# Two stacked blocks on one core: the recurrence's root as Ln and Exp on ScalarE, pieces of two gates exchanged, and x in the queue of the weights

## What is computed

```python
h = _rmsnorm(x, g_mix[l])                       # first block
y_xa = _memory_cross_attention(xa_q, _rmsnorm(mem, g_mem[l]), w_mem_kv[l], xa_g_q[l], xa_g_k[l])
...
for l in range(DEPTH_2):                        # second block
    h = x @ w_in[l]
    (hg_q, hg_f, hg_i, hg_gate, mla_cq, mla_ckv, mla_kr, mla_gate, mem_q, mem_gate) = jnp.split(h, IN_OFFSETS, axis=-1)
    ...
    y = jnp.concatenate([y_hg * jax.nn.silu(hg_gate), y_mla * jax.nn.silu(mla_gate), y_mem * jax.nn.silu(mem_gate)], axis=-1)
    x = _layernorm(DEEPNORM_ALPHA * x + y @ w_out[l], ln_g[l], ln_b[l])

# y_hg, with lb the layer's lower bound, 8 heads of 128
logf = jax.nn.log_sigmoid(z) + jnp.log1p(lb * jnp.exp(-z))
k = (1.0 - lb) * jax.nn.sigmoid(-z)
o = _chunk_gated_recurrence(q32, k, v, logf)    # v is hg_i
o = o * lax.rsqrt(jnp.mean(o * o, axis=-1, keepdims=True) + RMS_EPS)
```

## Time and profile before

| | us |
|---|---|
| median of 3 runs | 1149.06 (1148.51 to 1149.32) |
| the profiled execution | 1149.22, its span 1147.4 |
| PE busy | 1061.4 (93%) |
| DVE busy | 750.1 (65%) |
| ACT busy | 639.1 (56%) |
| granted PE clock, mean of the span | 0.966 of 2.4 GHz |

### The profile page before, as it was taken

The page is one execution under the profiler, slowest core; times in us unless marked ns, Lnnn a source line. Parts: engine busy times, 40 slices in busy tenths (PEclk is TensorE's granted clock), DMA queues, the critical chain, the costliest instruction groups (busy, mean ns, idle before and its releaser), DMA issues.

```text
span 1147.4 us, 19085 instructions
## 1 busy us (share of the span) xinstructions
PE 1061.4 (93%) x8070; PEld 943.4 (82%) x8070; DVE 750.1 (65%) x1070; ACT 639.1 (56%) x910; POOL 13.2 (1%) x18
## 2 busy tenths in 40 slices
PE   5799999999999999998999998896999999979975
PEld 4698987888879999987999997574899999957654
DVE  3575685885555878753646576669875564675786
ACT  4766565564464655543565678543356657784430
POOL 1000000000000000000000000100000000010000
PEclk9899998999999999999899999998999999998988
DMA  9553433566455565572546433222455463432110
GB/s 327 160 181 113 130 125 114 183 202 197 152 161 188 165 198 171 183 231 81 189 147 193 147 111 127 94 75 74 148 175 153 131 186 126 146 128 75 57 56 37
DMA packets 97688, 167.52 MB, mean 146 GB/s; under 512 B 7033, under 2 KB 32515, under 8 KB 97347
## 3 DMA queue, kind: packets, MB, share of 16 engines
q1 hardware_dynamic: 95216, 158.13, 43.1%
q0 software_dynamic: 1472, 5.51, 1.4%
q10 hardware_dynamic: 914, 2.67, 0.6%
HBM read 165.23 MB, written 1.05 MB: 145 GB/s over the span
## 4 chain that ended last, share of the span: by engine, by line
PE 80%; DVE 8%; ACT 7%; issue 2%; DMA 1%; ACTq 0%; DVEq 0%
PE proj L577 12%; PE proj L578 12%; PE proj L579 12%; PE proj L568 11%; PE proj L569 10%; PE proj L570 10%; ACT whi L985 2%; PE mix L881 1%; PE mix L590 1%; DVE arena L1895 1%; DVE wlo L1419 1%; PE mix L912 1%; PE mix L615 1%; PE mix L598 1%; ACT arena L1336 1%
## 5 line engine op out<-in xcount | busy, mean ns | idle before, releaser
L1419 DVE TENSOR_TENSOR wlo<-raw,whi 128x1024 fp32r<-128x1024 f32 (+3 forms) x303 | 355.1, 1202 | 198.6 <-ACT whi L985 197.2
L985 ACT ACTIVATE whi<-raw 128x1024 fp32r<-128x1024 f32 (+3 forms) x303 | 305.1, 1039 | 157.7 <-PE proj L579 70.7
L568 PE MATMUL proj<-act_hi,whi 128*128 128x256 f32 x1056 | 303.9, 288 | 7.8 <-DVE wlo L1419 4.2
L569 PE MATMUL proj<-act_lo,whi 128*128 128x256 f32 x1056 | 300.8, 285 | 0.0
L570 PE MATMUL proj<-act_hi,wlo 128*128 128x256 f32 x1056 | 300.8, 285 | 0.0
L568 PEld LDWEIGHTS proj<-act_hi,whi 128*128 128x128 f32 x1056 | 204.5, 194 | 9.8 <-DVE wlo L1419 4.4
L569 PEld LDWEIGHTS proj<-act_lo,whi 128*128 128x128 f32 x1056 | 204.6, 194 | 0.3
L570 PEld LDWEIGHTS proj<-act_hi,wlo 128*128 128x128 f32 x1056 | 204.5, 194 | 0.0
L577 PE MATMUL proj<-whi,y_hi 128*128 128x512 f32 (+1 forms) x352 | 141.9, 403 | 20.4 <-DVE X L1477 16.3
L578 PE MATMUL proj<-wlo,y_hi 128*128 128x512 f32 (+1 forms) x352 | 138.3, 393 | 0.0
L579 PE MATMUL proj<-whi,y_lo 128*128 128x512 f32 (+1 forms) x352 | 138.3, 393 | 0.0
(11 more groups left out here) (341 smaller groups left out, 1229.4 us busy)
## 6 DMA issues: line engine op xcount, KB each, us to landing
raw<-in_w_in SPq DMA_DIRECT2D x144, 512.0 KB, 4.4
raw<-in_w_up SPq DMA_DIRECT2D x88, 256.0 KB, 3.9
raw<-in_w_out SPq DMA_DIRECT2D x32, 512.0 KB, 3.6
raw<-in_w_down SPq DMA_DIRECT2D x22, 512.0 KB, 4.9
raw<-in_w_mem_kv SPq DMA_DIRECT2D x8, 512.0 KB, 9.4
raw<-in_w_mem_k SPq DMA_DIRECT2D x8, 512.0 KB, 3.8
raw<-in_w_o SPq DMA_DIRECT2D x8, 512.0 KB, 4.4
raw<-in_w_mem_v SPq DMA_DIRECT2D x8, 512.0 KB, 3.9
```

What stands on the lines that cost most here:

```text
L568: mm(o, wh[:, i, wc], hi[:, k0 + i, :], start=begin and j % 2 == 0, stop=False, skip_group_check=True)
L569: mm(o, wh[:, i, wc], lo[:, k0 + i, :], start=False, stop=False, skip_group_check=True)
L985: fn(whi[c % SPLIT][:, 0:w], raw[c % SLOTS][:, 0:w], ACT.Copy).then_inc(s.w_hi, 1)
L1419: tt(wlo[c % SPLIT][:, 0:w], raw[c % SLOTS][:, 0:w], f32(whi[c % SPLIT][:, 0:w]), ALU.subtract).then_inc(s.w_lo, 1)
```

## The change

Four things are moved, and one computation takes another form.

1. SP issues identity, mem, four pieces, x, and the other pieces; ACT issues the large constants only when x has landed, and POOL waits for x and no longer for mem. ACT squares mem behind piece 1 and x behind piece 3, and the first split before the root ends at piece 4.
2. hgi is projected ahead of hgg. hgi0 leaves its bank before the forget values' exponentials, hgi1 behind their Ln; hgg0 and hgg1 both leave in unit 3. |u| is formed on DVE in two halves (max of u and -u) behind the second latent output.
3. Keys 2 to 7 are made in pairs behind the splits of units 0 to 2.
4. mlaout1's first piece stands ahead of the last unit's products; gated(0) moves from unit 3 to unit 4; square(3) stands ahead of a split, and the split for mlaout1 on DVE behind both scales.
5. The root of the head norm is exp(-0.5 ln(.)) on ACT, for heads 0 to 3 within unit 6, and DVE only multiplies.

The diff, with context and empty lines left out:

```diff
@@ -147,7 +147,7 @@
                ("uk", [piece(a["w_mla_uk_2"][L], 0, 1, 0, 512)]), ("uv", [piece(a["w_mla_uv_2"][L], 0, 1, 0, 512)])]
-    groups += [(name, hg[name]) for name in ("hgf0", "hgf1", "hgq1", "hgg0", "hgg1", "hgi0", "hgi1")]
+    groups += [(name, hg[name]) for name in ("hgf0", "hgf1", "hgq1", "hgi0", "hgi1", "hgg0", "hgg1")]
@@ -494,10 +494,12 @@
         def _(sp):
+            sp.dma_start(const[:, 0:P], a["const"][:, 0:P]).then_inc(s.ident_in, 16)
+            for b in range(NB):
+                sp.dma_start(MEM[:, b, :], a["mem"][0, b * P:(b + 1) * P]).then_inc(s.mem_in, 16)
             for c, loads in enumerate(pieces):
-                if c == 1:
-                    for b in range(NB):
-                        sp.dma_start(MEM[:, b, :], a["mem"][0, b * P:(b + 1) * P]).then_inc(s.mem_in, 16)
+                if c == SLOTS:
+                    sp.dma_start(X[:, :, :], a["x"][0].rearrange("(b p) d -> p b d", p=P)).then_inc(s.x_in, 16)
                 if c >= SLOTS:
@@ -513,7 +515,7 @@
         def _(pool):
-            pool.wait_ge(s.mem_in, 32)
+            pool.wait_ge(s.x_in, 16)
             pool.dma_start(TREE_IN[:, :], a["tree"]).then_inc(s.tree_in, 16)
@@ -841,21 +843,21 @@
-                project("hgg0", L, act_hi, act_lo, part=(0, 1))
+                project("hgi0", L, act_hi, act_lo, part=(0, 1))
...
-                project("hgg0", L, act_hi, act_lo, part=(1, 2))
+                project("hgi0", L, act_hi, act_lo, part=(1, 2))
...
-                project("hgg0", L, act_hi, act_lo, part=(2, 4))
-                project("hgg1", L, act_hi, act_lo, part=(0, 2))
+                project("hgi0", L, act_hi, act_lo, part=(2, 4))
+                project("hgi1", L, act_hi, act_lo, part=(0, 2))
...
-                project("hgg1", L, act_hi, act_lo, part=(2, 3))
+                project("hgi1", L, act_hi, act_lo, part=(2, 3))
...
-                project("hgg1", L, act_hi, act_lo, part=(3, 4))
-                project("hgi0", L, act_hi, act_lo, part=(0, 3))
+                project("hgi1", L, act_hi, act_lo, part=(3, 4))
+                project("hgg0", L, act_hi, act_lo, part=(0, 3))
@@ -865,7 +867,7 @@
-                        project("hgi0", L, act_hi, act_lo, part=(3, 4))
+                        project("hgg0", L, act_hi, act_lo, part=(3, 4))
@@ -944,15 +946,16 @@
-                        project("hgi1", L, act_hi, act_lo, part=(u, u + 1))
+                        project("hgg1", L, act_hi, act_lo, part=(u, u + 1))
...
+                    if u == 7:
+                        project("mlaout1", L, y_hi, y_lo, 8, part=(0, 1))
...
-                project("mlaout1", L, y_hi, y_lo, 8, part=(0, 1))
@@ -1043,8 +1046,6 @@
-            act.dma_start(const[:, 0:P], a["const"][:, 0:P]).then_inc(s.ident_in, 16)
-            act.dma_start(X[:, :, :], a["x"][0].rearrange("(b p) d -> p b d", p=P)).then_inc(s.x_in, 16)
@@ -1057,21 +1058,23 @@
-            act.dma_start(const[:, P:], a["const"][:, P:]).then_inc(s.consts, 16)
...
-            split_until(SPLIT)
+            split_until(2)
...
+            split_until(SLOTS)
...
+            act.dma_start(const[:, P:], a["const"][:, P:]).then_inc(s.consts, 16)
...
+            split_until(SLOTS + 1)
@@ -1295,25 +1298,24 @@
-                split_until(ahead_of("hgg0", L, 1))
+                split_until(ahead_of("hgi0", L, 1))
...
-                leave("hgg0", L, HGT[:, 0:4, :], ACT.Silu)
+                split_until(ahead_of("hgi1", L, 0))
...
-                split_until(ahead_of("hgg1", L, 2))
+                split_until(ahead_of("hgi1", L, 2))
...
-                act.wait_ge(s.hg_u, L + 1)
+                leave("hgi0", L, HV[:, :, 0:512])
...
-                for h in quarter:
-                    last = fn(HX[:, h, :], HU[:, h, :], ACT.Abs)
-                link(last)
-                leave("hgg1", L, HGT[:, 4:8, :], ACT.Silu)
-                for h in quarter:
+                for n, h in enumerate(quarter):
+                    act.wait_ge(s.hg_u, 2 * L + n + 1)
...
+                nc.scalar.preload_act_table(ACT.Exp)
+                leave("hgi1", L, HV[:, :, 512:1024])
@@ -1355,42 +1357,55 @@
-                split_until(ahead_of("hgi0", L, 1))
+                def logs(dst, src):
+
+                    return fn(dst, src, ACT.Ln, bias=epsb[:, 0:1], scale=1.0 / HG_D)
+
+                def roots(dst):
+
+                    return fn(dst, dst, ACT.Exp, scale=-0.5)
+
+                split_until(ahead_of("hgg0", L, 1))
...
-                split_until(ahead_of("hgi0", L, 2))
+                split_until(ahead_of("hgg0", L, 2))
...
-                keys(2, 8)
-                leave("hgi0", L, HV[:, :, 0:512])
...
-                        split_until(ahead_of("hgi1", L, u))
+                        split_until(ahead_of("hgg1", L, u))
+                        keys(2 * u + 2, 2 * u + 4)
...
-                        leave("hgi1", L, HV[:, :, 512:1024])
+                        leave("hgg0", L, HGT[:, 0:4, :], ACT.Silu)
+                        leave("hgg1", L, HGT[:, 4:8, :], ACT.Silu)
+                        nc.scalar.preload_act_table(ACT.Exp)
...
+                    if u == 6:
+                        act.wait_ge(*out_of("hgo1", L))
+                        link(logs(HKT[:, 0:4, :], HKT[:, 0:4, :]))
+                        roots(HKT[:, 0:4, :]).then_inc(s.hg_r, 2)
...
-                root = lambda dst, src: fn(dst, src, ACT.Sqrt, bias=epsb[:, 0:1], scale=1.0 / HG_D)
-                act.wait_ge(*out_of("hgo1", L))
-                root(HKT[:, 0:4, :], HKT[:, 0:4, :]).then_inc(s.hg_r, 2)
...
-                root(pair_of(HKT, 2), pair_bank(2)[:, 1, :].rearrange("p (h t) -> p h t", h=2)).then_inc(out_of("hgo2", L)[0], 1)
+                logs(pair_of(HKT, 2), pair_bank(2)[:, 1, :].rearrange("p (h t) -> p h t", h=2)).then_inc(out_of("hgo2", L)[0], 1)
+                act.wait_ge(*out_of("hgo2", L))
+                roots(pair_of(HKT, 2)).then_inc(s.hg_r, 1)
...
+                square(3)
...
-                square(3)
...
-                root(pair_of(HKT, 3), pair_bank(3)[:, 1, :].rearrange("p (h t) -> p h t", h=2)).then_inc(s.hg_r, 1)
+                link(logs(pair_of(HKT, 3), pair_bank(3)[:, 1, :].rearrange("p (h t) -> p h t", h=2)))
+                roots(pair_of(HKT, 3)).then_inc(s.hg_r, 1)
@@ -1811,31 +1826,33 @@
-                split_until(ahead_of("hgg0", L, 1))
+                split_until(ahead_of("hgi0", L, 1))
...
-                last.then_inc(s.hg_u, 1)
+                link(last)
...
-                split_until(ahead_of("hgg0", L, 3))
-                split_until(ahead_of("hgg1", L, 1))
+                split_until(ahead_of("hgi1", L, 0))
...
+                dve.wait_ge(*stage(4, L))
+                for half in range(2):
+                    h = slice(4 * half, 4 * half + 4)
+                    stt(HX[:, h, :], HU[:, h, :], -1.0, HU[:, h, :], ALU.mult, ALU.max).then_inc(s.hg_u, 1)
...
-                dve.wait_ge(s.hg_u, L + 1)
-                split_until(ahead_of("hgg1", L, 3))
+                split_until(ahead_of("hgi1", L, 2))
...
-                split_until(ahead_of("hgi0", L, 1))
+                split_until(ahead_of("hgg0", L, 1))
...
-                split_until(ahead_of("hgi0", L, 2))
+                split_until(ahead_of("hgg0", L, 2))
@@ -1886,14 +1903,9 @@
-                    if p == 2:
-                        dve.wait_ge(*out_of("hgo2", L))
-                    else:
-                        dve.wait_ge(s.hg_r, 3 * L + (3 if p == 3 else 2))
+                    dve.wait_ge(s.hg_r, 4 * L + max(p + 1, 2))
...
-                    r = pair_of(HKT, p)
-                    link(nc.vector.reciprocal(r, r))
-                    stt(pair_of(HQT, p), pair_of(HQT, p), cur[:, 0:1], r, ALU.mult, ALU.mult).then_inc(s.hg_y, 1)
+                    stt(pair_of(HQT, p), pair_of(HQT, p), cur[:, 0:1], pair_of(HKT, p), ALU.mult, ALU.mult).then_inc(s.hg_y, 1)
@@ -1909,21 +1921,22 @@
-                        split_until(ahead_of("hgi1", L, u))
+                        split_until(ahead_of("hgg1", L, u))
...
-                    if u in (3, 5, 7):
-                        if u == 3:
-                            dve.wait_ge(*out_of("hgg0", L))
-                            dve.wait_ge(*out_of("hgg1", L))
+                    if u == 4:
+                        dve.wait_ge(*out_of("hgg0", L))
+                        dve.wait_ge(*out_of("hgg1", L))
+                        gated(0)
+                    if u in (5, 7):
...
-                split_until(ahead_of("mlaout1", L, 0))
...
+                split_until(ahead_of("mlaout1", L, 0))
```

## The result

The changed kernel takes 1114.2 us (median; 1113.3 to 1117.3) where the kernel before takes 1148.9, a ratio of 0.970 with a 95% interval of 0.969 to 0.971. The forecast was 1113.6. The profiled execution of the changed kernel has a span of 1111.5 us against 1147.4, so 35.9 us went in it; the sum of the prediction was 35.4.

The account below looks back on a forecast made before the run. PE, busy 93% of the span, was taken as the bound, with only its idle time to win. Terms 8.7 + 7.9 + 5.6 + 9.1 + 4.1 = 35.4 us off 1149.2 gave 1113.8, or 1113.6 as median; range 1106 to 1123.

Parts of the forecast that it names:

- The start: First transfers: x in SP's queue behind four pieces lets PE turn x at 26.7 instead of 35.37, gain 8.7 us.
- rival 1: First transfers: the single queue is slow, x lands at 25, the start gives 2.4 instead of 8.7: 1119.9 us; chance 0.10.
- The middle: Unit loops: hgi first, |u| on DVE and keys in pairs bring the third decays 8.9 and 10.2 us earlier.
- The new wait: Ahead of the first decays: three splits on DVE delay the logs' lower halves, costing PE 1.65 us of idle.
- Part 4: Work pushed into the units (hgg pieces, Silu and Exp loads, bank copies): cost 1.0 us, leaving 7.9 and 9.1 per layer.
- Rival 2: Ahead of the decays: DVE is next, its wait grows and each layer keeps half the middle's gain: 1123 us; chance 0.12.
- The roots: Layer ends: Ln and Exp on ACT replace reciprocals, hgout0 starts earlier, gain 5.6 us in the first layer, 4.1 in the second.
- delays diagonal(3) by 2.4: Second layer's end: mlaout1's piece ahead of the last products delays diagonal(3) by 2.4 us, so the gain is 4.1.
- Rival 3: Both layers: a table load costs its row's 1.28 us again, 4.4 us in all: 1118.0 us; chance 0.03.
- Rival 4: Gain beyond the count: PE's clock does not fall after shorter idles, second layer's 1.95 us stall goes: 1108 us; chance 0.09.
- Rival 5: Layer ends: X waits for weights or DVE's other work, not reciprocals; both ends give 1 at most: 1121.5 us; chance 0.03.
- Rival 6: Unit loops: new waits hold PE's clock at 1.2 GHz, some 60 us slower in all: 1174 us; chance 0.02.

Follow-up runs that it names:

- e_notree: Changed kernel loading only 128 of the tree's 2048 columns, the rest zeroed by GpSimd (results not the reference's): 1109.9 us in one run.
- a_xfirst: Changed kernel with DVE adding mlaout1 to X straight behind the two scales, both splits behind lower(2), ACT rounding pair 2 ahead of its split: 1106.6 us.
- a_logs: Changed kernel with ACT rounding the first half of the logs behind one split and DVE forming their lower halves behind one split, not three: 1110.9 us.
- a_tables: Changed kernel with two further table loads (Sqrt, then Exp) in each layer behind square(3), ahead of the split for which X waits: 1120.2 us.
- a_late: Changed kernel with constants issued behind the splits of xav's pieces, the tree and POOL's rows only when the sixth piece is split: 1117.4 us.
- p_roots: Kernel before with only exp(-ln/2) roots on ACT, mlaout1's first piece ahead of the last products, and DVE splits behind the scales: 12.3 us gained in its layers.
- b_xfirst: Kernel before, reciprocals and Sqrt kept, with DVE adding mlaout1 to X behind the first reciprocal and scale, ahead of splits and second reciprocal: 1145.2 us.
- p_keys: Kernel before with only six keys moved from between the first and second unit to follow in pairs: first to third decays 3.7 and 5.1 us less.

## Why the prediction was right, step by step

**The start: right at its place, too large at the end.** Forecast for x: landed at 14.3, squares at 18.7, turned by PE at 26.7. In the trace, as the answer to the earlier trace rows:

```profile
8.24 1.28 ACT L988 ACT_TABLE_LOAD   x1 [8.24 <-DMA raw<-in_w_mem_kv]
...
10.49 3.01 ACT L1021 ACTIVATE y_hi<-mix,cols 128x256 fp32r<-128x256 f32 x8
...
18.47 1.04 ACT L1075 ACTIVATE arena<-X 128x1024 f32<-128x1024 f32 x1
...
26.53 1.94 PE L592 MATMUL mix<-const,arena 128*128 128x128 f32 x16 [0.90 <-DVE arena L1440]
```

x landed at 15.4, 1.1 late, and nobody noticed, since the chain to the squares runs over ACT's splits and not over x. The turn of x is 8.8 us earlier, with 8.7 forecast. The step that failed is that the constants and the tree "cost nothing", with pieces 4 to 8 in by 27.6, worked out from one rate of 0.4 MB per us from 14.3 us on. They are not on the path themselves, but pieces 5 to 7 share the DMA engines with them and landed between 29.2 and 33.0, and piece 8 at 34.3. In the stretch from 16 to 24 us all queues together moved 226 GB/s and not 400 (stretch, its length, busy time and in brackets instructions of PE, its weight loads, DVE, ACT and POOL, then granted clock, DMA share, GB/s):

```profile
16.00:24.00 8.00, 8.00 (x35) 6.58 (x34) 3.91 (x4) 7.89 (x12) 3.02 (x6) 0.95 0.88 226
```

Bytes alone do not explain the rate: in e_notree, without the tree, it is 224 GB/s in the same stretch, and in the kernel before, with the tree, 372. Why is open. Of the 8.8 us 7.1 are left where the transposes of the keys begin (66.30 against 73.44) and 6.8 at the layers. That place no longer hangs on x: in a_xfirst, a_logs and a_tables PE turned x 0.7 to 1.6 us later than in the changed kernel, and the transposes of the keys begin at 66.46, 66.83 and 66.26, at most 0.5 later. This also settles rival 1: the single queue was not slow.

**The middle.** In the first layer the first forget transposes had no wait in front, as forecast; the third decays, forecast 8.9 us earlier, came 8.6 earlier, counted from the layer's own start, and 9.9 instead of 10.2 in the second.

```profile
691.80 0.39 PE L570 MATMUL proj<-act_hi,whi 128*128 128x256 f32 x1 [0.29 <-ACT arena L999]
700.52 1.04 PE L867 MATMUL mix<-const,arena 128*128 128x128 f32 x8
...
707.12 0.50 PE L883 MATMUL mix<-tree_r,y_hi 128*128 128x512 f32 x1 [1.83 <-DVE y_lo L1854]
```

The new wait was forecast at 1.65 and is 1.83; the bank's was put at 0.5 and is 0.3. With 6.8 added, the decays stand at 713.9 on the axis of the earlier trace rows, against 713.65. Part 4 cost 0.9 and 1.2 instead of 1.0 (to the decays of the last unit). So 7.6 and 8.6 arrive for 7.9 and 9.1. Rival 2, DVE next, was right about the place and wrong about the size.

**The roots.** From the last products to hgout0 the forecast was 11.0 us and the trace has 10.7 (780.87 - 770.17); the remaining wait, forecast at 4 to 5, is 4.0, with X as its end. Beyond what start and middle gave, hgout0 starts 6.0 us earlier, for 5.6. What was left out came behind it: after 8.1 us of idle the matmuls of the kernel before ran at 0.63 us for 5.3 us, after 4.0 us of idle for 3.0 us, which is another 1.0. In the second layer the same interval gives 5.9 for 4.1. The step that failed there is "delays diagonal(3) by 2.4": it does, but in the kernel before the granted clock was 0.77 between 1088 and 1093, and in the changed kernel 1.00 in the same stage (1057 to 1062), which gave 1.4 back. So this term was too small by 1.5 and 1.8, as the start was too large by 1.9 and the middle by 0.3 and 0.5: the terms of the 35.4 us were mis-sized in both directions and cancel. That the forecast of 1113.6 lies 0.6 from the median is luck in that respect; the mechanisms and places are what it had right.

**The other rivals.** Rival 3 falls by a_tables. Rival 4 is half right: behind both new waits of 1.8 us the clock was 1.00 in the changed kernel, though in the first layer of a_late, a_xfirst and a_tables it was 0.66 behind the same wait; behind the 4.0 us for X it fell, and the second layer's odd stall is still there (L883 <- issue: 2.0 us in which PE waited for nothing that the profile shows). Rival 5 falls by size, since p_roots gave 6.1 and 6.2 and not 1, and b_xfirst shows that order alone does not give it; but of the 4.0 us that were left, 3.2 were DVE's other work, as it said. Rival 6 falls by the clock, 0.98 over the span.

## What to carry to other kernels

A wait names the instruction that ended it, not the ones queued ahead of that instruction: here half of the time from the scales to hgout0 (3.2 of 6.5 us) was left to splits that PE wanted only some pieces later, and reordering them was worth 7.6 us, as much as a part of the change. Transfers that nobody waits for still move beside others that somebody waits for; when they are moved, ask which piece stands beside them now. And a part that shortens a wait behind which the clock fell can be worth more than the wait: taking 2.5 us of keys off ACT's path gave 3.7 and 5.1 us.

## What the runs showed of the hardware

The code from PE's wait of 1.5 us near 100 us to the layers is the same in all these kernels, and yet its length differs by up to 5.4 us between executions: 539.5 us in p_roots, 544.9 in the changed kernel (544.6 in the kernel before, so these two can be compared). PE waits 2.7 us at one place and 3.4 at another there, within a hundredth alike in every trace; whether the granted clock falls behind them is not. One stretch of 5 us behind the first wait in the kernel before and in p_roots (columns as above, the third from the end is the granted clock):

```profile
305.00:310.00 5.00, 4.73 (x14) 3.81 (x15) 1.35 (x2) 0.11 (x2) 0.00 (x0) 0.66 0.27 105
```

```profile
305.00:310.00 5.00, 5.00 (x24) 4.12 (x23) 1.58 (x2) 1.06 (x1) 0.00 (x0) 1.00 0.29 108
```

In p_keys it was 0.50 there, the lower of the clock's two levels (1.2 GHz) throughout.

In the thirteen traces the clock stayed at 1.00 for the 8 us behind the first wait in two, and behind the second in six. That is why p_roots, with 12.3 us gained in its layers, shows 16.7 in its profiled execution, and why differences of 2 to 3 us between these kernels were read from stages of the traces and not from the medians.
